# Key projection of the mLSTM mixer replaced by a per-head product of the query and key weights

## What is computed

```
q = einsum("bshd,hde->bhse", heads(xconv), w_qkv[0])
k = einsum("bshd,hde->bhse", heads(xconv), w_qkv[1]) * 128 ** -0.5
v = einsum("bshd,hde->bhse", heads(xm),    w_qkv[2])
# q and k are used only in products with each other:
s   = einsum("bhctd,bhcsd->bhcts", qc, kc) * w_intra          # scores in a chunk
C_k = einsum("bhcsd,bhcse->bhcde", vc * w, kc)                # chunk states
num = s @ v + w_inter * einsum("bhcde,bhcte->bhctd", C_prev, qc)
```

## Time and profile before

| what | value |
| --- | --- |
| three runs | 2495.97, 2498.97, 2498.82 us |
| median of the runs | 2498.82 us |
| span of the profiled execution | 2494.0 us |
| instructions in it | 35459 |
| busy: PE, PEld | 97%, 89% of the span |
| busy: DVE, ACT, POOL | 75%, 45%, 25% |
| granted TensorE clock, mean | 0.997 of full speed |
| heads of the mixer of layer 0 | about 688.7 to 785 us of the span |
| heads of the mixer of layer 1 | about 1990.6 to 2069 us |

### The profile page before, as it was taken

How to read it: one execution, slowest core, us unless ns; L and a number is a source line. 1 busy time by engine, 2 the same in 40 slices (tenths; PEclk the granted TensorE clock), 3 DMA queues, 4 the chain that set the end, 5 groups by cost and what they waited for, 6 DMA issues and landing times.

```text
span 2494.0 us, 35459 instructions
## 1 busy us (share of the span) xinstructions
PE 2427.1 (97%) x13552; PEld 2208.6 (89%) x13552; DVE 1874.1 (75%) x2362; ACT 1126.9 (45%) x1627; POOL 611.6 (25%) x429
## 2 busy tenths in 40 slices
PE   7999999999999999999999999999999998899998
PEld 4999998888977899999888999999889777899987
DVE  5799997776567779988766799876556677898733
ACT  5334443444453743443354544443444555555522
POOL 0344440000500034544000145541000500266400
PEclk9999999999999999999999999999999999999999
DMA  6333336543111343333643423346443203322331
GB/s 258 110 127 127 140 135 256 186 148 94 52 48 36 118 160 122 129 111 132 247 161 135 169 110 126 130 156 242 180 142 101 89 28 118 136 101 101 119 118 67
DMA packets 100369, 328.33 MB, mean 132 GB/s; under 512 B 7810, under 2 KB 38050, under 8 KB 86946
## 3 DMA queue, kind: packets, MB, share of 16 engines
q1 hardware_dynamic: 83040, 316.33, 35.5%
q10 hardware_dynamic: 17218, 10.55, 1.4%
HBM read 318.28 MB, written 8.57 MB: 131 GB/s over the span
## 4 chain that ended last, share of the span: by engine, by line
PE 78%; DVE 12%; issue 5%; ACT 3%; DMA 2%; POOL 0%; SPq 0%; ACTq 0%; DVEq 0%; POOLq 0%
PE ps L2206 29%; PE ps L2166 27%; PE ps L2154 8%; PE ps L928 6%; DVE junk L1764 3%; DVE w_all L2014 2%; DMA acc<-w_ada_t 1%; DVE w_all L1744 1%; PE ps L2248 1%; PE ps L997 1%; PE ps L1068 1%; PE ps L1044 1%; PE ps L2258 1%; PE ps L952 1%; PE ps L1055 1%
## 5 line engine op out<-in xcount | busy, mean ns | idle before, releaser
L2206 PE MATMUL ps<-w_all,hj_all 128*128 128x512 f32 x2856 | 655.6, 391 | 4.9 <-DVE arena L828 2.5
L2206 PEld LDWEIGHTS ps<-w_all,hj_all 128*128 128x128 f32 x2856 | 535.1, 188 | 117.9 <-DVE arena L828 2.9
L2166 PE MATMUL ps<-xn_hi,w_all 128*128 128x384 f32 (+1 forms) x2592 | 612.2, 318 | 12.0 <-DVE gate_row L2067 11.1
L1744 DVE TENSOR_TENSOR w_all<-raw,w_all 128x2048 fp32r<-128x2048 f32 x138 | 322.0, 2333 | 268.8 <-ACT w_all L1387 268.7
L2166 PEld LDWEIGHTS ps<-xn_hi,w_all 128*128 128x128 f32 x2592 | 449.3, 189 | 18.9 <-DVE gate_row L2067 18.0
L2166 PE MATMUL ps<-xn_lo,w_all 128*128 128x384 f32 (+1 forms) x1296 | 411.0, 317 | 0.0
L1387 ACT ACTIVATE w_all<-raw 128x2048 fp32r<-128x2048 f32 x139 | 262.6, 1889 | 241.4 <-PE ps L2206 206.1
L2014 DVE TENSOR_TENSOR w_all<-raw,w_all 128x1024 fp32r<-128x1024 f32 (+1 forms) x216 | 329.9, 1529 | 36.5 <-ACT w_all L1609 36.2
L1764 DVE SCALAR_TENSOR_TENSOR junk<-acc,silu_row 128x1024 bf16<-128x1024 f32 x224 | 325.7, 1454 | 16.4 <-DMA acc<-w_ada_t 7.1
L1609 ACT ACTIVATE w_all<-raw 128x1024 fp32r<-128x1024 f32 (+1 forms) x216 | 197.9, 918 | 261.1 <-PE ps L2166 241.9
L2154 PE MATMUL ps<-xn_hi,w_all 128*128 128x384 f32 (+1 forms) x1024 | 245.7, 324 | 9.9 <-DVE xn_lo L1822 7.6
(11 more groups left out here) (236 smaller groups left out, 3213.0 us busy)
## 6 DMA issues: line engine op xcount, KB each, us to landing
raw<-w_ff_in SPq DMA_DIRECT2D x104, 1024.0 KB, 4.9
raw<-w_ff_out SPq DMA_DIRECT2D x77, 1024.0 KB, 5.0
acc<-w_ada_t SPq DMA_DIRECT2D x128, 512.0 KB, 3.3
raw<-w_out SPq DMA_DIRECT2D x16, 1024.0 KB, 4.9
raw<-w_in SPq DMA_DIRECT2D x12, 1024.0 KB, 5.7
x<-x_in SPq DMA_DIRECT2D x12, 512.0 KB, 10.7
gate_row<-gate_out_rows ACTq DMA_DIRECT2D x12, 512.0 KB, 6.4
x_out<-x SPq DMA_DIRECT2D x12, 512.0 KB, 9.0
```

Of the source, the lines that this page charges most:

```text
L1744: nc.vector.tensor_tensor(w_lo[par][:, 0:width], raw[par][:, 0:width], w_hi[par][:, 0:width].bitcast(F32), ALU.subtract).then_inc(S["w_lo" ...
L2166: ins = mm(ps[:, bank_, 0:xx[0].shape[-1]], w[:, c], x_[:, k, :], start=start and k == 0 and a == 0, stop=k == 3 and a == 2, skip_group_ch ...
L2206: ins = mm(ps[:, 2 * i + hf, :], xx[:, i * P:(i + 1) * P], w[:, c, hf * 512:(hf + 1) * 512], start=first and c == 0 and a == 0, stop=last ...
```

## The change

The host hands over the query and key weights transposed (heads' matrices as e by d), the value weights as before. Between chunk 5 and chunk 6 PE multiplies them for all four heads into bank 6, and ACT writes the scaled product over the query weights. `project(h, 1)` now makes the values, `project(h, 2)` the transposes of the convolved features, and `project(h, 3)` and `kT` are gone. `likeness` takes `convT` in the place of `kT`.

```
@@ mixer_act
             split(6)
+            act.wait_ge(S["qk_mm"], m + 1)
+            nc.scalar.activation(qkv_w[:, 0].rearrange("p h e -> p (h e)"), ps[:, 6, :], ACT.Copy,
+                                 scale=float(HD) ** -0.5).then_inc(S["qk_sb"], 1)
             act.wait_ge(S["g_m"], m + 1)
...
-                dst, b0 = ((qT, 2), (kT, 4), (ktok, 2), (vtok, 4))[a]
-                act.wait_ge(S["qkv_mm"], 4 * (4 * m + h) + a + 1)
+                dst, b0 = ((qT, 2), (vtok, 4), (ktok, 2))[a]
+                act.wait_ge(S["qkv_mm"], 3 * (4 * m + h) + a + 1)
...
                 project(h, 2)
-                project(h, 3)
                 if h == 0:
                     split(8)
@@ mixer_dve, values
-                    dve.wait_ge(S["qkv_sb"], 4 * (4 * m + h) + 4)
+                    dve.wait_ge(S["qkv_sb"], 3 * (4 * m + h) + 2)
@@ mixer_pe
             mm(ps[0:1, 7, 160:224], ones[:, 0:1], lfs..., start=True, stop=True).then_inc(S["g_b"], 1)
+            for h in range(HEADS):
+                ins = mm(ps[:, 6, h * P:(h + 1) * P], qkv_w[:, 0, h, :], qkv_w[:, 1, h, :], start=True, stop=True)
+            ins.then_inc(S["qk_mm"], 1)
             chunk(6, out_groups)
...
-                k, b0 = 4 * m + h, (2, 4, 2, 4)[a]
-                if a >= 2:
-                    pe.wait_ge(S["qkv_sb"], 4 * k + a - 1)
+                k, b0 = 4 * m + h, (2, 4, 2)[a]
+                if a == 2:
+                    pe.wait_ge(S["qkv_sb"], 3 * k + 1)
                 elif h:
                     pe.wait_ge(S[("inter_rd", "comb")[a]], 2 * k - 1)
                 for g in range(2):
+                    if a == 0:
+                        w = len(outs[g]) * P
+                        ins = mm(ps[:, b0 + g, 0:w], qkv_w[:, 0, h, :], convT[:, h, g * GW:g * GW + w], ...)
+                    for t in range(g * GT, (g + 1) * GT) if a else ():
+                        dst = ps[:, b0 + g, (t % GT) * P:(t % GT + 1) * P]
+                        if a == 1:
+                            ins = mm(dst, xmT[:, h, t * P:(t + 1) * P], qkv_w[:, 2, h, :], start=True, stop=True)
+                        else:
+                            ins = nc.tensor.transpose(dst, convT[:, h, t * P:(t + 1) * P], ident[:])
...
@@ likeness
-                pe.wait_ge(S["qkv_sb"], 4 * k + 2)
+                pe.wait_ge(S["qkv_sb"], 3 * k + 1)
-                    ins = mm(ps[:, t // GT, ...], kT[:, sl], qT[:, sl], start=True, stop=True)
+                    ins = mm(ps[:, t // GT, ...], convT[:, h, sl], qT[:, sl], start=True, stop=True)
@@ the heads' loop
+            pe.wait_ge(S["qk_sb"], m + 1)
             for h in range(HEADS):
...
                 project(h, 2)
-                project(h, 3)
                 likeness(h)
```

More of the change, by code:

```diff
@@ L387, in head @@
             return small(n, "head", XN)
-        qT, kT = head(TOK), head(TOK)
+        qT = head(TOK)
         ktok = head(TOK).rearrange("p (t n) -> p t n", t=NT)
@@ L415, in build @@
             "lead_mm lead_sb win_evac mix_const g_cp g_tok g_abs g_exp g_ln g_lf g_b g_r g_rT g_rmx g_rr g_m g_dec g_bc g_rows g_T g_arg g_w nm_hi nm_lo nm_st nm_in nm_sel "
-            "ab_mm ab_sb fold folded xab_mm xab_sb f_mm f_sb conv conv_silu "
+            "qk_mm qk_sb ab_mm ab_sb fold folded xab_mm xab_sb f_mm f_sb conv conv_silu "
             "qkv_mm qkv_sb st_mm mb_mm wt_sb wv_sb cloc_mm cst_sb p_sb inter_mm inter_rd io_mm comb hvar hstd hn hnT mix_done"
@@ L589, in project @@
                     src = ps[:, b0 + g, 0:w]
-                    if a < 2:
+                    if a == 0:
                         to = dst[:, g * GW:g * GW + w]
@@ L594, in project @@
                         src = src.rearrange("p (t n) -> p t n", n=P)
-                    ins = nc.scalar.activation(to, src, ACT.Copy, scale=float(HD) ** -0.5 if a in (1, 2) else 1.0)
+                    ins = nc.scalar.activation(to, src, ACT.Copy)
                 ins.then_inc(S["qkv_sb"], 1)
@@ L994, in project @@
                 for g in range(2):
[L995 to L1002, removed]
+                    if a == 0:
+                        w = len(outs[g]) * P
+                        ins = mm(ps[:, b0 + g, 0:w], qkv_w[:, 0, h, :], convT[:, h, g * GW:g * GW + w], start=True, stop=True)
+                    for t in range(g * GT, (g + 1) * GT) if a else ():
[4 more added lines that the diff above has]
+                            ins = nc.tensor.transpose(dst, convT[:, h, t * P:(t + 1) * P], ident[:])
                 ins.then_inc(S["qkv_mm"], 1)
@@ L1008, in maxima @@
                 if d == 0:
-                    pe.wait_ge(S["qkv_sb"], 4 * k + 3)
+                    pe.wait_ge(S["qkv_sb"], 3 * k + 3)
                     if h == 0:
@@ L1027, in likeness @@
                     pe.wait_ge(S["comb"], 2 * k)
-                pe.wait_ge(S["qkv_sb"], 4 * k + 2)
+                pe.wait_ge(S["qkv_sb"], 3 * k + 1)
                 for t in outs[0] + outs[1]:
                     sl = slice(t * P, (t + 1) * P)
-                    ins = mm(ps[:, t // GT, (t % GT) * P:(t % GT + 1) * P], kT[:, sl], qT[:, sl], start=True, stop=True)
+                    ins = mm(ps[:, t // GT, (t % GT) * P:(t % GT + 1) * P], convT[:, h, sl], qT[:, sl], start=True, stop=True)
                 ins.then_inc(S["st_mm"], 1)
@@ L1038, in added @@
                 if d == 0:
-                    pe.wait_ge(S["qkv_sb"], 2 * md + 4)
+                    pe.wait_ge(S["qkv_sb"], 3 * (4 * m + h) + 3)
                 else:
@@ L2413 @@
         "w_out": np.asarray(w_out),
-        "w_qkv": np.asarray(w_qkv),
+        "w_qkv": np.stack([np.asarray(w_qkv)[:, 0].swapaxes(-1, -2), np.asarray(w_qkv)[:, 1].swapaxes(-1, -2),
+                           np.asarray(w_qkv)[:, 2]], 1),
                 "cvec_in": np.ascontiguousarray(np.stack([np.asarray(c)[0], np.asarray(c_ctx)]).reshape(2, KC, P).transpose(2, 1, 0)),
```

## The result

The changed kernel takes 2508.29 us (median of 4 runs, 2503.32 to 2510.08), the kernel before 2498.89 us on the same chip (4 runs, 2495.97 to 2500.07). The ratio is 1.0039, with a 95% interval of 1.0026 to 1.0053. Slower by 0.39%: the forecast had been 2501.5 us and a range up to 2506.8. So the loss is real, 9 to 10 us, though PE has 64 matmul records fewer. The profiled executions are the shortest of the four in both kernels (2503.32 us with a span of 2501.5 after; before, by its span of 2494.0, the one of 2495.97): the profiles can explain 7.5 us, and the medians are 9.4 us apart.

A forecast was written before the change was run, and what follows sets the result against it. In heads 1 to 3 it took the detour over ACT and DVE as the bound (PE level in layer 1). Terms +1.8, -1.9, -0.1, +0.1, +0.1 gave 0.0; clock falls +2.7 and span to median +4.8 gave 2501.5 us, range 2495.2 to 2506.8.

The forecast's parts named there:

- the detour over ACT and DVE: After `transform`: `xab` evacuation, table load, square root, DVE's norm, then `head_out`; not shortened, so PE waits 2.3 to 2.4 us (layer 0).
- Head 0 of layer 0: ACT's path to its split gets shorter until the slot's load lands at 695.89: gain 1.9 us.
- The product: Four f32 matmuls on PE between two chunks: 0.9 us in each mixer, 1.8 us in all, bounds 0 and 2.6.
- The rival that the saving counts in full: Each head 1.99 us shorter if `head_out` does not wait for the root: 14.1 us, 2484.7 us; chance 0.06.
- The rival that the transposes cost as much as the matmuls: Holes ahead of `head_out` 0.7 us shorter, with fewer clock falls, 2499 us; chance 0.03.
- a fall of 3.4 us thus costs up to 1.7 us: PE at half clock for 3.4 us loses up to 1.7 us, nearly all where PE is the path, behind `head_out`.
- clock falls in most heads: Behind `head_out` in heads 1 to 3 and head 0 of layer 1: at most 11.9 us, 2510.7 us; chance 0.22.
- The chances of a fall: 0.65 in head 0 of layer 1, 0.4 per later head of layer 0, 0.2 of layer 1; likeliest 2.7 us.
- none behind shorter ones: Falls seen only behind PE waits of 2 us or more; waits of 1.85 and 0.59 us brought none.
- head 0 of layer 1: The slot's load, landing at 1998.22, limits ACT's split: gain at most 0.1 us, PE waits about 3.8 us.
- the bare sum: Whole kernel without clock falls: terms sum to 0.0 us, 2498.8 us; chance 0.27 together with the case of 2495.2 us.
- The last term, +4.8 us from span to median: Whole kernel: the old median stands 4.8 us above the old span; added to the forecast span of 2496.7.

The follow-up runs named there:

- e4: Changed kernel with a one-column square root on ACT at the start of heads 1 to 3, so its table loads early; 2496.28 us, ratio 1.0000.
- e6: Kernel before with three useless ACT copies (2.1 us) ahead of the square root of heads 1 to 3; 2518.73 us, ratio 1.0098.
- e10: Kernel before with the product of the weights added on PE, its result unused; 2498.16 us, ratio 1.0018.
- e3: Changed kernel with four useless matmuls ahead of `head_out` in heads 1 to 3; 2496.87 us, ratio to the kernel before 1.0007.
- e9: e5 without the early load of the square root's table, so the new order alone; 2497.21 us, ratio 1.0011.
- e8: e5 with `head_out` placed between `maxima(h, 0)` and `added(h, 0)`; 2488.41 us, ratio 0.9970.
- e1: Changed kernel with nine useless matmuls ahead of `head_out` in heads 1 to 3; 2497.36 us, ratio to the kernel before 1.0004.
- e2: Changed kernel with 18 useless transposes ahead of `head_out` in heads 1 to 3; 2496.12 us, ratio to the kernel before 0.9998.
- e5: Changed kernel with early table load and three engines reordered, so PE does `maxima` and `added(h, 0)` during the norm; 2486.19 us, ratio 0.9966.

## Why the prediction was wrong

**What held.** That the detour over ACT and DVE and not PE sets heads 1 to 3: forecast a wait of 2.3 to 2.4 us released by L858 and a head of 23.6 us; measured 2.41 us, released by the same line, and 23.62 us. e4 (detour shorter, head shorter by 0.65) and e6 (detour longer by about 2.1, head longer by 2.06) show it from both sides. The values ahead of `transform`: +0.045 forecast, +0.05 measured. Head 0 of layer 0: -1.9 forecast, -2.04 measured, in part by luck (see below). The product: 0.9 forecast in each mixer, 0.88 and 0.79 measured, and e10 alone 0.87 and 0.81. The rival that the saving counts in full fell: none of the heads 1 to 3 became 21.6 us. The rival that the transposes cost as much as the matmuls fell too.

**What failed: the price of a fall.** The step "a fall of 3.4 us thus costs up to 1.7 us" rested on two rows of the kernel before. Behind the new holes the low stretch was 6.8 us each time, and it cost 2.54 to 3.05 us, not 1.6. I had forecast one or two falls in the heads, 2.7 us; there were three, at 2.9 us on average, 8.6 us. By the count alone, three at 1.6 would be 4.8 us; the price brought the other 3.8. Where a low stretch of 3.4 us did come in a head (e3, e4, e6, e9), it cost 1.3 to 1.7 us, about as forecast: what was mis-sized is the length. The kernel before itself has a low stretch twice as long at its start, of which the earlier trace rows hold only the last 3.1 us:

```profile
41.70:48.40 6.70, 2.94 (x9) 2.94 (x10) 3.94 (x7) 6.60 (x13) 1.14 (x1) 0.50 0.46 159
```

It would have shown that 3.4 us is not the only length, and that the price of a fall goes to about 3.4 us.

**What failed: how many.** The rival "clock falls in most heads" was the one that came nearest, with a chance of 0.22 and a condition of four falls. Three were enough at this price. The chances of a fall (0.4 and 0.2 a hole) took layer 1's holes, of about 2.0 us, as much safer than layer 0's; layer 1 had two of the three. And "none behind shorter ones", which I read from one wait of 1.85 us and one of 0.59, is wrong in general: falls came behind 1.86 (e3, e8), 1.85, 1.76 and 1.28 (e4) and 1.43 us (e3), and none behind two of the three waits of 2.41 us.

**What failed: head 0 of layer 1.** Forecast of the head -0.1 and a wait of 3.8 us with a likely fall; measured -2.04, a wait of 1.85 us and no fall. In the changed kernel:

```profile
1997.26 9.03 SPq L1153 DMA_DIRECT2D raw<-w_out  x2
...
2001.63 1.91 ACT L1393 ACTIVATE w_all<-raw 128x2048 fp32r<-128x2048 f32 x1
...
2003.57 2.29 DVE L1750 TENSOR_TENSOR w_all<-raw,w_all 128x2048 fp32r<-128x2048 f32 x1 [1.89 <-ACT w_all L1393]
...
2007.80 1.35 PE L1050 MATMUL ps<-arena 128*128 128x129 f32 x10 [1.85 <-DVE arena L797]
```

ACT's split starts 4.4 us behind the issue of that load, which needs 6.2 us to land. So it is not the load that this split reads. I had matched the two in the earlier trace rows because 1991.92 + 6.3 fell 0.09 us before the start of the split: a coincidence. The data of the slot that it does read did not hold it up, and the whole of the two saved us counted, as in layer 0. This error made the forecast of the bare sum 1.9 us too high and put a fall where none came, so it hid a part of the first error. In layer 0 the forecast had the same wrong limit: in the changed kernel that load is issued at 692.54 and lands 6.1 us later, at 698.63, and the split starts at 698.48, before it. The -1.9 came out near because ACT's own path, worked out beside it, gave nearly the same time.

**The sum once more**, with what was measured: +1.7 (product) - 4.1 (head 0, twice) + 0.2 + 8.6 (three falls) = +6.4 us, of 7.5 us of span. The rest of the span, +1.2 us, lies outside the heads. There the low stretches differ from run to run: the changed kernel has one of 10.2 us at its start for 6.8 us before, and one from 800.3, and none where the earlier trace rows show one at 2109. e6 has the same long stretch at the start (38.6 to 48.9) with the old code there, so it is no effect of the changed code of the start.

**The last term, +4.8 us from span to median,** came out at 6.8 (2508.29 - 2501.53). It is no fixed cost: each profiled execution takes 1.8 to 2.0 us more than its own span, and the rest is how far the median lies above the shortest execution. The other three executions of the changed kernel have a mean granted clock of 0.989 to 0.990, the profiled one 0.992, so they spent more time at the lower level. Whether in the heads or outside them no profile shows.

**Why e1 and e2 are only at parity,** though their heads and the product sum to 2.5 us less than before, has the same likely answer. The mean granted clock is 0.994 in e1 and e2 (medians of 12 and 11 executions) and 0.996 in the 35 of the kernel before beside them. As an estimate from these figures, that is some 10 us more at the lower level, more than enough for 2.5 us at the price seen in the heads. Their profiles have such falls behind the heads (2158.7 and 2182.6 in e1, for example). Why they are there is open.

## What to carry to other kernels

Work taken off an engine that already waits at the end of a step becomes a longer wait, and on PE such a wait is not free: it can bring the low clock, which here cost 2.5 to 3 us for a hole of 2.0 to 2.4 us. Shorten the detour that sets the step (e4), or move other work into the hole (e5), before counting a saving; where neither can be done, useless matmuls in the hole lengthened no head and kept the clock up in the heads (e1, e2). When a price is read from rows, look for all stretches of the kind, not the two nearest, and match a load with its reader by the slot and not by the time. And a profile is one execution: see where it stands among the others before its falls are counted.

## What the runs showed of the hardware that was not expected

- Low stretches of the clock were 3.4, 6.8 or 10.2 us long. In the heads those of 3.4 us cost 1.3 to 1.7 us, those of 6.8 us 2.5 to 3.2 us, where PE sets the time.
- Whether the clock falls behind a given wait is not set by that wait alone: in the two profiles of the changed kernel 2.4 us brought a fall in two of six holes and 2.05 us in four of six; in e6 2.39 us did in one of three and 2.04 us in three of three. The wait of 1.85 or 1.86 us in head 0 of layer 1, which all twelve profiles of the study have, was followed by a fall in three of the twelve (e3, e4, e8). 1.43 us brought one in three, and what was left of the holes in e1 and e2 (0.31 and 0.36 us in layer 0) none.
- Eighteen f32 transposes in the hole held the clock as well as nine f32 matmuls (18 records): 1.00 over all heads in both.
- The table load could be taken off the path by a square root of one column ahead of it, which took 0.65 us off a head whose detour had 1.28 us of table load in it.
